# A gate kept in PSUM, and one vector product moved ahead of a weight split, in a feed-forward pipeline

## The reference, cut to what matters

```python
h = h + 0.5 * swiglu(rmsnorm(h, ffn1_norm), w_gate, w_up, w_down)   # 528 tokens
...
h = h + 0.5 * swiglu(rmsnorm(h, ffn2_norm), w_gate, w_up, w_down)   # 512 tokens are used
def swiglu(x, w_gate, w_up, w_down):                                 # hidden width 2816 = 22 x 128
    return (silu(x @ w_gate) * (x @ w_up)) @ w_down
```

## Time and profile before

| | |
|---|---|
| median of 3 runs | 2088.42 us (2087.04 to 2089.91) |
| the profiled execution | 2086.18 us, span 2084.2 us |
| PE busy | 2014.4 us, 97% |
| PEld busy | 1760.0 us, 84% |
| DVE busy | 1099.2 us, 53% |
| ACT busy | 839.0 us, 40% |
| POOL busy | 600.0 us, 29% |

### The profile page before, as it was taken

One profiled execution on the slowest core, in us unless ns is written; L12 is line 12 of the kernel. 1 busy time (PEld: TensorE's weight loads), 2 busy tenths in 40 slices (PEclk: granted clock), 3 DMA queues, 4 the chain that ended last, 5 costly groups with the idle time before them and its releaser, 6 DMA issues.

```text
span 2084.2 us, 33869 instructions
## 1 busy us (share of the span) xinstructions
PE 2014.4 (97%) x14432; PEld 1760.0 (84%) x14432; DVE 1099.2 (53%) x1618; ACT 839.0 (40%) x1330; POOL 600.0 (29%) x207
## 2 busy tenths in 40 slices
PE   8999999999999998999999999999999999999998
PEld 6899888878977788999999878898777787989897
DVE  4400575246257738765565252266566547747473
ACT  5332232336456534443434344342222334434353
POOL 4443332544320134120202422045243234020202
PEclk9999999999999999999999999999999999999999
DMA  5323121322311120323232431122013131333321
GB/s 176 101 82 111 56 76 61 101 75 80 99 61 41 42 81 27 116 82 115 83 107 82 103 101 31 50 80 76 28 63 113 62 101 53 125 99 99 110 88 56
DMA packets 170063, 171.64 MB, mean 82 GB/s; under 512 B 16941, under 2 KB 160681, under 8 KB 169913
## 3 DMA queue, kind: packets, MB, share of 16 engines
q1 hardware_dynamic: 168508, 167.25, 25.5%
q10 hardware_dynamic: 1404, 2.23, 0.3%
HBM read 163.17 MB, written 6.29 MB: 81 GB/s over the span
## 4 chain that ended last, share of the span: by engine, by line
PE 83%; DVE 8%; issue 4%; ACT 3%; POOL 1%; DMA 1%; ACTq 0%; SPq 0%; DVEq 0%; POOLq 0%
PE ps L2362 81%; PE ps L2364 2%; DVE normed L1816 1%; DVE w_lo L1808 1%; DVE sg L1865 1%; DVE w_sum_lo L1798 0%; DVE tmp L1892 0%; ACT w_hi L927 0%; DMA x_rows<-in_x 0%; ACT diag L985 0%; DVE mla_q L2030 0%; DVE gdn_x L2227 0%; POOL w_lo L784 0%; DVE gdn_inv_t L2210 0%; DVE tmp L1531 0%
## 5 line engine op out<-in xcount | busy, mean ns | idle before, releaser
L784 POOL TENSOR_TENSOR w_lo<-w_raw,w_hi 128x2048 fp32r<-128x2048 f32 (+2 forms) x117 | 493.9, 4224 | 1035.7 <-ACT w_hi L927 596.2
L2362 PE MATMUL ps<-u_hi,w_hi 128*128 128x512 f32 (+2 forms) x1480 | 477.3, 343 | 13.3 <-DVE tmp L1860 3.5
L2362 PE MATMUL ps<-u_hi,w_lo 128*128 128x512 f32 (+2 forms) x1472 | 470.2, 339 | 0.0
L2362 PE MATMUL ps<-u_lo,w_hi 128*128 128x512 f32 (+2 forms) x1472 | 462.7, 339 | 1.0 <-DVE u_lo L1519 0.8
L2362 PEld LDWEIGHTS ps<-u_hi,w_hi 128*128 128x128 f32 x1480 | 267.7, 189 | 43.8 <-issue 5.5
L2362 PEld LDWEIGHTS ps<-u_lo,w_hi 128*128 128x128 f32 x1472 | 265.0, 189 | 31.1 <-DVE u_lo L1519 5.4
L2362 PEld LDWEIGHTS ps<-u_hi,w_lo 128*128 128x128 f32 x1472 | 266.4, 189 | 27.8 <-issue 0.5
L927 ACT ACTIVATE w_hi<-w_raw 128x2048 fp32r<-128x2048 f32 (+2 forms) x157 | 248.0, 1581 | 65.6 <-PE ps L2362 59.6
L2362 PE MATMUL ps<-hidden_hi,w_hi 128*128 128x264 f32 (+1 forms) x528 | 141.6, 322 | 2.8 <-DVE hidden_lo L1849 2.8
L2362 PE MATMUL ps<-hidden_lo,w_hi 128*128 128x264 f32 (+1 forms) x528 | 141.5, 322 | 0.0
L2362 PE MATMUL ps<-hidden_hi,w_lo 128*128 128x264 f32 (+1 forms) x528 | 141.1, 321 | 0.0
(11 more groups left out here) (423 smaller groups left out, 4012.0 us busy)
## 6 DMA issues: line engine op xcount, KB each, us to landing
w_raw<-in_w_in_a SPq DMA_DIRECT2D x22, 1024.0 KB, 5.1
w_raw<-in_ffn_w_gate SPq DMA_DIRECT2D x22, 1024.0 KB, 5.3
w_raw<-in_ffn_w_up SPq DMA_DIRECT2D x22, 1024.0 KB, 5.3
w_raw<-in_ffn_w_down SPq DMA_DIRECT2D x24, 768.0 KB, 4.4
w_raw<-in_w_in SPq DMA_DIRECT2D x17, 1024.0 KB, 5.3
w_raw<-in_w_out_a SPq DMA_DIRECT2D x8, 1024.0 KB, 5.1
w_raw<-in_w_kv SPq DMA_DIRECT2D x8, 1024.0 KB, 5.4
w_raw<-in_w_in_b SPq DMA_DIRECT2D x8, 1024.0 KB, 5.3
```

What stands on the lines that cost most here:

```text
L784: pool.tensor_tensor(WL[:, u % RAWS, part], RAW[:, u % RAWS, part], WH[:, u % SPLITS, part].bitcast(F32), ALU.subtract).then_inc(lo_done, 1)
L2362: return nc.tensor.matmul(o, a, b, start=start, stop=stop, **kw)
```

## The change

In up units of seven products that are followed by another such unit, VectorE's program takes `hidden_out(0)` ahead of `last_rows_lo`; before, it stood behind it. In plain gate units the product with RSTDB is written back into the accumulator in PSUM instead of `sg`, ScalarE takes silu there in place, and the second product with RSTDB reads PSUM and writes `sg`. The slot is freed by this second product; before, it was freed by the first. ScalarE waits for `silu_scaled`, which the first product now raises, and VectorE's wait at the end of the gate unit is for the two slots. The number of instructions on each engine stays as it was.

```diff
@@ ffn_act, plain_unit
                     for m in range(2):
                         slot, uses = chunk_of(jg, 0, j, m)
-                        act.wait_ge(ps_free[slot], uses + 1)
                         if j % 2 == 0:
-                            nc.scalar.activation(SG[:, m, 0:width], SG[:, m, 0:width], ACT.Silu).then_inc(silu_done, 1)
+                            act.wait_ge(silu_scaled, 4 * number + j + m + 1)
+                            nc.scalar.activation(acc(slot, width), acc(slot, width), ACT.Silu).then_inc(silu_done, 1)
                         else:
+                            act.wait_ge(ps_free[slot], uses + 1)
                             nc.scalar.activation(HH[:, 2 * (j // 2) + m, 0:width], TMP[:, m, 0:width], ACT.Copy).then_inc(hh_done, 1)
@@ ffn_dve, plain_unit
                         if j % 2 == 0:
-                            nc.vector.tensor_tensor(halves(SG[:, m, 0:width]), acc(slot, width), halves(RSTDB[:, 0:width]),
-                                                    ALU.mult).then_inc(ps_free[slot], 1)
+                            nc.vector.tensor_tensor(acc(slot, width), halves(RSTDB[:, 0:width]), acc(slot, width),
+                                                    ALU.mult).then_inc(silu_scaled, 1)
...
                         if j % 2 == 0:
                             dve.wait_ge(silu_done, 16 + 4 * number + j + m + 1)
-                            nc.vector.tensor_tensor(SG[:, m, 0:width], SG[:, m, 0:width], RSTDB[:, 0:width],
-                                                    ALU.mult).then_inc(silu_scaled, 1)
+                            slot, uses = chunk_of(jg, 0, j, m)
+                            nc.vector.tensor_tensor(halves(SG[:, m, 0:width]), halves(RSTDB[:, 0:width]), acc(slot, width),
+                                                    ALU.mult).then_inc(ps_free[slot], 1)
                         else:
                             hidden_low(0, j // 2, m, 2 * (j // 2) + m + 1)
                     if j % 2 == 0:
-                        dve.wait_ge(silu_scaled, 4 * number + j + 2)
+                        for m in range(2):
+                            slot, uses = chunk_of(jg, 0, j, m)
+                            dve.wait_ge(ps_free[slot], uses + 1)
@@ ffn_dve, seven_unit
                     if u + 1 in seven_no:
                         summed_lo(u + 1)
-                        last_rows_lo(u + 1)
                     if up:
                         dve.wait_ge(done, unit_ticks[u])
                         hidden_out(0)
+                    if u + 1 in seven_no:
+                        last_rows_lo(u + 1)
```

## The result

The changed kernel took 2070.24 us (median of 5 runs, 2069.16 to 2073.45) where the kernel before took 2088.85 beside it (5 runs, 2087.04 to 2089.91): ratio 0.9917, 95% interval 0.9906 to 0.9929, or 17.3 us off (15 to 20); the two medians alone differ by 18.6. The forecast was 2072.1, from 2068 to 2078. The profiled execution took 2070.14 us, its span 2068.1.

The account below looks back on a forecast made before the run. TensorE, busy for 97% of the span, was taken as the bound, so only its gaps or clock could give time. 12.0 + 1.7 + 2.6 = 16.3 us off 2086.18, plus 2.2 for the median, gave 2072.1 us, range 2068 to 2078.

Parts of the forecast that it names:

- only shift: Stages between the two feed-forward networks: chained to TensorE's end, they start earlier but keep their length.
- The product moved ahead: Twelve crossings between up units: emptying pair 0 earlier lets the seed copy come in time and closes p6's gap, 12.0 us.
- ffn2's p7: ffn2's six crossings: p7 waits for its seed copy L1221, 0.2 plus 0.1 for a slow first matmul, 0.3 each.
- The gate in ffn2: ffn2's plain units: L1860 comes 1.0 earlier, TensorE's gap of 2.76 becomes 1.7, the clock stays up; 2.6 us, ends 0 to 2.7.
- The gate in ffn1: ffn1's plain units: L1860 1.4 us earlier, fourth accumulator 1.74 later, half clock behind a 3.35 gap; 1.7 us won.
- the step that puts the half clock of before behind the gap of 3.48: ffn1's plain units: the clock fell behind the 3.48 us gap, and its half clock cost 1.5 us.
- (1): Rival: crossing gaps close but plain units return nothing, through GpSimd's splits or falls of the clock; 2076.4 us, chance 0.13.
- (2): Rival: a new wait replaces the removed one, p7 behind L1221 or VectorE's added products; 2078.1 us, chance 0.12.
- (3): Rival: the move does nothing, the seed waits for something unnamed, and plain units' gains are lost; about 2088 us, chance 0.06.
- (4): Rival: VectorE waits for its unit's end, making product, rounding and p6's seed late; 2094.9 us, chance 0.02.

Follow-up runs that it names:

- the move alone: Kernel before with only VectorE's hidden_out(0) put ahead of last_rows_lo, plain units' gates unchanged: 2075.05 us against 2087.50, ratio 0.9938.
- the late rounding: Kernel before with ScalarE's rounding of pair 0 placed behind the next seven-product unit's first two seeds, VectorE's order unchanged: 2074.54 us against 2087.50, ratio 0.9937.
- the gate alone: Changed kernel with VectorE's reorder undone, so only the plain units' gates stay in PSUM: 2083.97 us against 2087.50, ratio 0.9983.

## Why the prediction was right

The time was 1.9 us below the forecast, inside its own range, and the mechanism that it rested on holds at each step that a run could test but one, the place of the half clock in ffn1. What put the time below the forecast is the step from the profile to the median: the profiled execution took 2070.14 us where the sum gave 2069.9, but the median of the runs, which lay 2.2 us above the profiled one in the kernel before, lies 0.1 above it in the changed one. That the profile met the sum is luck in part. The stretches that the change touches gave 17.9 us, not 16.3, and the stages between the networks did not "only shift": they and the start took 1.9 back.

**The product moved ahead.** Right, and shown from two sides: reordering VectorE returns 12.9 us and reordering ScalarE 13.2. The working also had the spare time right: the seed leaves p6 0.10 us in ffn1 (888.81 + 0.51 against 889.42), where it had 0.11, and 0.02 in ffn2, where it had 0.03. The low part that is moved back has 1.5 us to spare for p2 (its end 889.36, p2 890.89), where the sum had 1.4. VectorE's wait for its own unit's end held up nothing.

The term that was mis-sized is ffn2's p7. I charged 0.3 for a new wait at each of 6 crossings; p7 starts 2.87 us behind p6, where 24 spacings make 2.83, and its first matmul takes 0.35 in place of 0.28: 0.1 in all. Two things made the wait smaller: L1222 started 2.42 us behind p6 where I had 2.51, and p7 followed it by 0.45 in place of 0.51. The crossings of ffn2 gave 1.09 each, not 0.9, and those of ffn1 1.07, not 1.1: 12.9 us in place of 12.0. The upper end of this term was added wrongly: without a new wait 6 x 1.1 + 6 x 1.2 is 13.8, not 13.2.

**The gate in ffn2.** Right in kind, 2.97 us in place of 2.6, and above the 2.7 that I gave as its end. L1861 came 1.44 us earlier relative to the first product of the network, not 1.0: 1.2 in unit 2, and 0.2 in the first unit, which the term had left out (two L1865 took 1.55 us there, two L1867 take 1.29). So the gap is 1.3 and not 1.7, and the clock stays up behind it in all five profiles that have this gate and this gap.

**The gate in ffn1.** The steps came as stated: 1.3 us for two products from PSUM, two normalise operations in the blocked places, L1861 1.53 us earlier (1.4 predicted), a gap of 3.29 (3.35 predicted) with half the clock behind it. In the pair of profiles it gave 2.05 where the term says 1.7. But the step that puts the half clock of before behind the gap of 3.48, as though it belonged there, failed: with the same code it fell behind the gap of 1.61 in the profiles with the move alone and with the late rounding, where the stretch took 60.3 and not 61.7 us. By the means of all profiles of either kind the term is 0.3, too large as forecast by 1.4; for the one execution that I worked from it was nearly right. The run of the gate alone, 3.5 us (1.7 to 5.4) for both networks, is too coarse to tell the two apart.

What I took from the Trainium skill (SBUF — State Buffer, "SBUF: two separate sides") agrees with the run that moved normalise's second input to PSUM: 5.49 us for eight in place of 10.94. The Trainium skill (TensorE: Matmul & The Clock Gate, "HAM oscillation — how this bites in real kernels") tells of a kernel whose waits between bursts are longer than 2.11 us and throttle the clock each time. Here half the clock followed the waits of 3.3 and 3.5 us in all six profiles that have one, which agrees. It followed the wait of 2.11 us in ten profiles and not in two, and that of 1.61 us in five of seven: falls come behind shorter waits too, but not each time.

**The rivals.** (1) falls with the 3.5 us of the gate alone, though in ffn1 it came close. (2) falls with p7 on time; that p7 is the next to be late is shown by the run that moved the product one step further. (3) falls with the move alone. (4) had the right wait and the wrong victim: where VectorE does stand waiting for the unit's end, what comes late is not p6 but the sums behind it, and p7 by 0.7 us.

The sum over all profiles is 12.9 + 3.0 + 0.3 = 16.2 us, against 17.3 (15 to 20) and 16.3 (14 to 19) measured; my 16.3 came from errors of +0.9, +0.4 and -1.4 that cancel, which is luck.

## What to carry to other kernels

When TensorE waits for a small copy, look at what stands ahead of that copy in its engine's queue and what that one waits for: the cure may be a reorder on either engine, and going one step too far only moves the wait to the next reader of the same queue. If a VectorE operation stretches beside GpSimd, give it one input in PSUM, but count what the longer stay in PSUM does to the accumulator that wants the slot. A cost of the half clock that is read from one profile belongs to that execution; read several before a term is built on it.

## What the hardware showed that I had not expected

The clock falls at different gaps from one execution to the next, with the same code: in ffn1's plain units behind 1.61 us in five profiles of seven, and in that of the kernel before behind 3.48 instead; between the networks behind 2.11 us in ten profiles of twelve. What decides it in one execution is open. The stretch between the networks, whose code is alike in the eleven profiles without added products there, took from 610.6 us, with half the clock for 3.4 us of it, to 615.1, with half the clock for 17.1, and was the longer the more of it ran at half the clock. That difference is larger than the whole gain in ffn1's plain units.

VectorE's operations with one input in PSUM took 0.66 to 0.69 us each, as the mean of a row of them, beside GpSimd's splits, whether they wrote SBUF or PSUM. GpSimd's two splits were a little shorter too, 9.12 us in place of 9.58, when normalise had one input in PSUM.
